# Opening of a conditioned hybrid layer: scale and shift made in two halves, conditioning blocks reordered, first projection weights split early

## What is computed (the reference, cut)

```python
mod = silu(c) @ w_ada + b_ada              # 9 conditioning rows (8 sample, 1 prompt), w_ada 1024 x 6144
sh1, sc1, g1, sh2, sc2, g2 = split(mod, 6)
h = rmsnorm(x, norm_mix_g) * (1 + sc1) + sh1
proj = h @ w_in                            # q, f, i, g, conv B, conv C, conv v, two merge gates
```

## Time and profile before

| what | value |
|---|---|
| median of three runs | 2126.03 us (2125.35 to 2129.06) |
| the profiled execution's own time | 2128.7 us |
| its span | 2127.1 us |
| mean granted clock of PE, share of full speed | 0.957 |
| PE busy over the span | 1928.6 us (91%) |
| DVE, ACT, POOL busy | 1044.8, 872.1, 414.0 us (49%, 41%, 19%) |

### The profile page before, as it was taken

The page is one execution under the profiler, slowest core; times in us unless marked ns, Lnnn a source line. Parts: engine busy times, 40 slices in busy tenths (PEclk is TensorE's granted clock), DMA queues, the critical chain, the costliest instruction groups (busy, mean ns, idle before and its releaser), DMA issues. The chain is left out here.

```text
span 2127.1 us, 33716 instructions
## 1 busy us (share of the span) xinstructions
PE 1928.6 (91%) x10176; PEld 1507.9 (71%) x10177; DVE 1044.8 (49%) x1519; ACT 872.1 (41%) x1181; POOL 414.0 (19%) x337
## 2 busy tenths in 40 slices
PE   3799999899899999989789999999899999999960
PEld 3799999899888666755446777666566777777740
DVE  3212411155337334545336666565566666666646
ACT  4210111234203222211246666666566666666642
POOL 0100000111111000001112333333233333223320
PEclk9899999999899999999899999999999999999985
DMA  6211221011263666325069999999999999979946
GB/s 240 71 50 40 82 96 30 30 60 43 68 209 117 216 219 212 138 86 195 19 257 380 306 292 294 356 318 379 374 327 345 286 286 286 275 233 310 279 91 259
DMA packets 154836, 433.67 MB, mean 204 GB/s; under 512 B 11551, under 2 KB 76307, under 8 KB 130210
## 3 DMA queue, kind: packets, MB, share of 16 engines
q1 hardware_dynamic: 120338, 307.40, 38.6%
q0 software_dynamic: 31776, 116.05, 21.1%
q10 hardware_dynamic: 2672, 9.57, 1.2%
HBM read 351.27 MB, written 81.72 MB: 204 GB/s over the span
## 5 line engine op out<-in xcount | busy, mean ns | idle before, releaser
L2038 DVE TENSOR_TENSOR wexp_lo<-wexp,wexp_hi 128x2048 fp32r<-128x2048 f32 x190 | 426.9, 2289 | 49.3 <-ACT wexp_hi L1990 44.4
L1990 ACT ACTIVATE wexp_hi<-wexp 128x2048 fp32r x190 | 353.2, 1907 | 54.4 <-issue 52.9
L1971 PE MATMUL bank<-wexp_down,hTe 128*128 x736 | 331.0, 592 | 1.8 <-ACT ob L2016 1.8
L1946 PE MATMUL bank<-wexp_hi,x_hi 128*128 128x512 f32 x744 | 300.0, 403 | 3.8 <-DVE wexp_lo L2038 3.8
L1946 PE MATMUL bank<-wexp_hi,x_lo 128*128 128x512 f32 x744 | 291.5, 392 | 0.0
L1946 PE MATMUL bank<-wexp_lo,x_hi 128*128 128x512 f32 x744 | 290.0, 390 | 0.0
L1920 POOL DMA_INDIRECT acc_d<-ob,ixs x92 | 153.0, 1663 | 599.8 <-DMA acc_d<-ob,ixs 290.9
L1971 PEld LDWEIGHTS bank<-wexp_down,hTe 128*128 128x128 f32 x736 | 138.8, 189 | 142.4 <-issue 135.5
L494 PE MATMUL bank<-hT_hi,w_hi 128*128 128x344 f32 x576 | 187.7, 326 | 3.3 <-DVE w_lo L578 3.3
L494 PE MATMUL bank<-hT_hi,w_lo 128*128 128x344 f32 x576 | 185.7, 322 | 0.0
L494 PE MATMUL bank<-hT_lo,w_hi 128*128 128x344 f32 x576 | 185.1, 321 | 0.0
(11 more groups left out here) (338 smaller groups left out, 2917.3 us busy)
## 6 DMA issues: line engine op xcount, KB each, us to landing
wexp<-in_w_exp_gate SPq DMA_DIRECT2D x64, 1024.0 KB
wexp<-in_w_exp_up SPq DMA_DIRECT2D x64, 1024.0 KB
wexp_down<-in_w_exp_down SPq DMA_DIRECT2D x64, 1024.0 KB
wada<-in_w_ada SPq DMA_DIRECT2D x12, 2048.0 KB, 10.9
w_raw<-in_w_in SPq DMA_DIRECT2D x44, 512.0 KB, 3.9
gates_d<-gst POOLq DMA_DIRECT2D x48, 172.0 KB, 2.1
gate<-gates_d SPq DMA_DIRECT2D x16, 516.0 KB, 5.5
xn<-in_x_prompt ACTq DMA_DIRECT2D x8, 512.0 KB
```

Source lines behind the costliest of these rows:

```text
L1946: last = pe.matmul(banks[0][:].rearrange("p (g n) -> p g n", g=2), stat[:, b, k, :], mov[:, b, :, k * FF:(k + 1) * FF], start=(k == 0 and ...
L1971: last = pe.matmul(banks[4 + half][:], hT[:, f, :], wdn[:, bass.ds(slot, 1), f, half * 512:half * 512 + 512].rearrange("p a n -> p (a n)") ...
L1990: act.activation(w_hi[:, b, g, :], wexp[:, bass.ds(e & (RING - 1), 1), g, :].rearrange("p a n -> p (a n)"), ACT.Copy).then_inc(whi_ok, 1)
L2038: dve.tensor_tensor(w_lo[:, b, g, :], wexp[:, bass.ds(e & (RING - 1), 1), g, :].rearrange("p a n -> p (a n)"), w_hi[:, b, g, :], ALU.subtr ...
```

## The change

It has five parts.
1. x squared tile by tile: each tile of x has its own semaphore, and ACT squares it as soon as it has landed.
2. Blocks of w_ada are loaded and used in the order 0, 2, 1, 3. The parameter rows are turned after the first of them, into another bank.
3. Scale and shift are made in two halves of four feature tiles. PE's order is: block 0, parameter rows, block 2, turn their mod tiles, feature tiles 0 and 1, block 1, feature tiles 2 and 3, block 3, turn its and block 1's mod tiles, the sample tokens, feature tiles 4 to 7. DVE and ACT take up the second half's scale and shift between feature tiles 3 and 4, and the sample tokens before the last two feature tiles.
4. The first 128 columns of w_in are loaded behind the last block of w_ada on SP's queue, rounded by POOL, and the subtraction is POOL's too. For that w_raw and the first two slots of w_hi and w_lo are allocated in the opening.
5. In `project_in` the first pass stands outside the loop, and the conv state is turned and copied after it, not before. The loop has one pass fewer.

The core of the diff:

```diff
+COLUMNS = (4, 5, 6, 3, 0, 1, 2)
...
+            BLOCKS = (0, 2, 1, 3)
...
-                    for n in range(2):
+                    for n in BLOCKS[0:2]:
                         sp.dma_start(wada[:, n], ada_v[:, :, n * 512:(n + 1) * 512]).then_inc(ada_in[n], 16)
...
-                    for n in range(2, FIRST):
+                    for n in BLOCKS[2:]:
                         sp.dma_start(wada[:, n], ada_v[:, :, n * 512:(n + 1) * 512]).then_inc(ada_in[n], 16)
+                    sp.dma_start(w_raw[:], w_in[:, :, COLUMNS[0] * W:COLUMNS[0] * W + P]).then_inc(w0_in, 16)
...
+                    pool.wait_ge(w0_in, 16)
+                    pool.tensor_copy(w_hi[0][:, 0], w_raw[:]).then_inc(w0_hi, 1)
+                    pool.wait_ge(w0_hi, 1)
+                    pool.tensor_tensor(w_lo[0][:, 0], w_raw[:], w_hi[0][:, 0], ALU.subtract).then_inc(w0_lo, 1)
...
-                    act.wait_ge(x_in, 16 * TILES)
                     for t in range(TILES):
+                        act.wait_ge(x_in[t], 16)
...
-                        if k + 1 < KD:
+                        if k + 1 < KD and k + 1 != KD // 2:
                             first_half(k + 1)
...
+                        if k + 1 == KD // 2:
+                            act.wait_ge(modT_ok, 2)
+                            first_half(k + 1)
+                        if k == 6:
+                            act.wait_ge(smp_ok, 1)
+                            act.activation(hT_hi[:, :, T:], hsmp[:], ACT.Copy).then_inc(smp_hi_ok, 1)
...
+                    cond(0)
+                    pe.wait_ge(par_in, 16 * 5)
+                    pe.transpose(banks[7][:, 0:NPAR], par_rows[:], ident[0:NPAR, 0:NPAR]).then_inc(par_T, 1)
+                    cond(1)
+                    turn_mod(0)
+                    pe.wait_ge(xn_ok, TILES)
+                    turn(0)
+                    turn(1)
+                    cond(2)
+                    turn(2)
+                    turn(3)
+                    cond(3)
+                    turn_mod(1)
...
+                    for k in range(4, KD):
+                        turn(k)
...
+                    condition_rows(0)
+                    condition_rows(1)
+                    shift_and_scale(0)
...
                     second_half(0)
                     for k in range(KD):
-                        if k + 1 < KD:
+                        if k + 1 == KD // 2:
+                            rest(k)
+                            condition_rows(3)
+                            shift_and_scale(1)
                             second_half(k + 1)
...
+                        else:
+                            if k + 1 < KD:
+                                second_half(k + 1)
+                            rest(k)
+                        if k == 1:
+                            condition_rows(2)
+                        if k == 4:
+                            dve.wait_ge(smp_ps, 1)
+                            s.link(dve.tensor_tensor(hsmp[:], banks[6][:, 0:KD * NS].rearrange("p (k c) -> p k c", c=NS),
+                                                     modT[:, KD:, 0:NS], ALU.mult))
+                            dve.tensor_tensor(hsmp[:], hsmp[:], modT[:, 0:KD, 0:NS], ALU.add).then_inc(smp_ok, 1)
```

and in `project_in`:

```diff
-            load(0)
             for u in range(1, UNITS + 1):
...
+            pool.sem_inc(hi_ok, 1)
+            for c in range(1, CH):
+                pool.wait_ge(raw_in, 16 * c)
+                pool.tensor_copy(w_hi[c // 2][:, c % 2], raw[:]).then_inc(hi_ok, 1)
+            with pool.Fori(1, PASSES) as i:
...
+            tensor_pass(0, 0)
             pe.wait_ge(cs_in, 16)
...
-            with pe.Fori(0, 6) as i:
+            with pe.Fori(1, 6) as i:
                 tensor_pass(i, i * PER)
...
-            for c in range(CH):
+            dve.sem_inc(w_ready, 1)
+            for c in range(1, CH):
                 rest(0, c)
```

More of the change, by code:

```diff
@@ L154, in layer @@
         hT_lo = sb("hT_lo", [P, KD, TT], F32R, split, "right")
+        w_raw = sb("w_raw", [P, KD, P], F32, split, "right")
+        early = top.enter_context(ExitStack())
+        w_hi = [sb("w_hi0", [P, 2, KD, P], F32R, early, "right")]
+        w_lo = [sb("w_lo0", [P, 2, KD, P], F32R, early, "right")]
         ada_v = a["w_ada"].rearrange("l (k p) n -> p (l k) n", p=P)
@@ L178, in layer @@
             rstd = sb("rstd", [P, TILES], ctx=c1)
-            par_in, c_in, b_in, x_in = sem("par_in"), sem("c_in"), sem("b_in"), sem("x_in")
+            par_in, c_in, b_in = sem("par_in"), sem("c_in"), sem("b_in")
+            x_in = [sem(f"x_in{t}") for t in range(TILES)]
+            w0_in, w0_hi, w0_lo = sem("w0_in"), sem("w0_hi"), sem("w0_lo")
             ada_in = [sem(f"ada_in{i}") for i in range(FIRST)]
@@ L186, in layer @@
             dve1, pool1 = sem("dve1"), sem("pool1")
[L187 removed]
+            smp_ps, smp_ok, smp_hi_ok, hi_ok, lo_ok = (sem(n) for n in ("smp_ps", "smp_ok", "smp_hi_ok", "hi_ok", "lo_ok"))
+            BLOCKS = (0, 2, 1, 3)
             O_G, O_LB, O_HG, O_CW, O_CB = 0, KD, KD + 2 * CH, KD + 2 * CH + H, KD + 2 * CH + H + 3 * CH
@@ L265, in _, with turn @@
                     pe.wait_ge(cT_cp, 1)
-                    def cond(n):
+                    def cond(x):
+                        n = BLOCKS[x]
                         pe.wait_ge(ada_in[n], 16)
[L269 to L284, removed]
+                        if x >= 2:
+                            pe.wait_ge(mod_ok, x - 1)
+                        condition(pe, banks[x % 2], wada[:, n]).then_inc(mod_ps, 1)
+                    def turn(k):
                         for half in range(2):
@@ L297, in _ @@
                                             ident[0:NS, 0:NS])
-                    last.then_inc(xT_ps, 1)
+                    last.then_inc(smp_ps, 1)
+                    for k in range(4, KD):
+                        turn(k)
                 @block.vector
@@ L316, in _ @@
                     dve.wait_ge(b_in, 64)
[L317 to L330, removed]
@@ L338, in second_half, with rest @@
                                           modT[:, k, NS:NS + 1], ALU.mult, ALU.add).then_inc(h_dve_ok, 1)
+                    def rest(k):
+                        dve.wait_ge(hi_ok, k + 1)
+                        dve.tensor_tensor(hT_lo[:, k, 0:T], hraw[:, k % 3, :], hT_hi[:, k, 0:T], ALU.subtract).then_inc(lo_ok, 1)
                     second_half(0)
                     for k in range(KD):
-                        if k + 1 < KD:
+                        if k + 1 == KD // 2:
+                            rest(k)
+                            condition_rows(3)
+                            shift_and_scale(1)
                             second_half(k + 1)
[L344 to L348, removed]
-                    dve.tensor_tensor(hsmp[:], hsmp[:], modT[:, 0:KD, 0:NS], ALU.add).then_inc(smp_ok, 1)
+                        else:
[9 more added lines that the diff above has]
+                            dve.tensor_tensor(hsmp[:], hsmp[:], modT[:, 0:KD, 0:NS], ALU.add).then_inc(smp_ok, 1)
                     dve.wait_ge(smp_hi_ok, 1)
@@ L373, in layer @@
                     project_in(nc, tidy, a, c4, sb, sem, banks, par, ident, w_in, hT_hi, hT_lo, qT, fT, gT, bT, vv, u_end, w_raw,
-                               g_d, b_d, (O_LB, O_CW, O_CB))
+                               w_hi, w_lo, g_d, b_d, (O_LB, O_CW, O_CB))
+                early.close()
                 next_stage()
@@ L426, in layer, with project_in @@
         final(nc, a, o, sb, sem, eps, mod_d, x2_d, acc_d)
-def project_in(nc, tidy, a, ctx, sb, sem, banks, par, ident, w_in, hT_hi, hT_lo, qT, fT, gT, bT, vv, u_end, raw, g_d, b_d, offsets):
+def project_in(nc, tidy, a, ctx, sb, sem, banks, par, ident, w_in, hT_hi, hT_lo, qT, fT, gT, bT, vv, u_end, raw, w_hi, w_lo,
+               g_d, b_d, offsets):
     O_LB, O_CW, O_CB = offsets
     cvT = sb("cvT", [P, CH, TT], ctx=ctx)
-    w_hi = sb("w_hi", [P, CH, KD, P], F32R, ctx)
-    w_lo = sb("w_lo", [P, CH, KD, P], F32R, ctx)
+    w_hi = w_hi + [sb("w_hi1", [P, 2, KD, P], F32R, ctx)]
+    w_lo = w_lo + [sb("w_lo1", [P, 2, KD, P], F32R, ctx)]
     cstT = sb("cstT", [P, CH, NS * 2], ctx=ctx)
@@ L497, in used @@
             def used(c, n=1):
-                pe.matmul(banks[7][:, 0:2], w_hi[:, c, 0, 0:P], w_hi[:, c, 0, 0:2], start=True, stop=True).then_inc(w_used, n)
+                one = w_hi[c // 2][:, c % 2, 0]
+                pe.matmul(banks[7][:, 0:2], one[:, 0:P], one[:, 0:2], start=True, stop=True).then_inc(w_used, n)
             def tensor_pass(i, first):
@@ L540, in _ @@
             act.activation(lbt[:, 0:2, :], lbt[:, 0:2, :], ACT.Exp).then_inc(lb_ok, 1)
-            act.wait_ge(cT_ps, 1)
-            act.activation(cstT[:].rearrange("p c n -> p (c n)"), banks[6][:, 0:CH * 2 * NS], ACT.Copy).then_inc(cT_ok, 1)
             def take(dst, func, first):
@@ L552, in _ @@
             take(bT, ACT.Copy, 0)
+            act.wait_ge(cT_ps, 1)
```

(1 more changed line is left out.)

33 lines of the change are left out of this document (18 added, 15 removed).

## The result

The changed kernel takes 2114.94 us (median of 4 runs, 2109.96 to 2119.33) against 2125.69 us for the kernel before: ratio 0.9946, interval 0.9928 to 0.9964. Measured a second time, together with some of the experiments, it came to 0.9946 again (0.9932 to 0.9959). That is about 11 us less, where 12.8 were forecast; the median forecast was 2113.2, in a range of 2110 to 2117. The profiled execution is the longest of the four: 2119.33 us.

The account below looks back on a forecast made before the run. The opening's chain (x, squares, xn, bias, blocks 2 and 3, modT, eight tiles, weights) sets project_in's first matmul, which carries everything behind it. -13.3 + 0.5 = -12.8 takes 2128.7 to 2115.9, median 2113.2; range 2110 to 2117.

Parts of the forecast that it names:

- The squares and xn: Opening, ACT and DVE: squares start as tiles land, ending near 21.9 and not 29.2; xn ends at 30.1.
- The rival of tiles landing together: Opening: tiles of x land nearly together, squares and xn end as before, everything 6.7 us later: 2119.9; chance 0.12.
- Half 0: Opening, first four feature tiles: scale and shift at 32.3, first hT_lo at 34.8, the fourth ending at 42.3.
- The 1.1 us lost on block 1: Opening, PE: block 1 takes 2.5 us, so tile 2 is turned at 37.1 where DVE wanted it at 36.0.
- the 0.3 us charged to DVE for POOL's subtraction: Opening: slowdown of DVE while POOL subtracts the first weights, 0.3 us with bounds 0 and 2.
- POOL's own length: Opening: POOL's 128x1024 subtraction takes 2.7 to 13.4 us by elements; the low end and a little more was taken.
- The last rival: Opening: POOL and DVE hold each other up, six hT_lo each cost 4.8 us more: 28.8, giving 2142; chance 0.02.
- Half 1: Opening, last four feature tiles: modT at 43.7, first hT_lo at 47.0, the eighth ending at 53.7, opening ending at 53.9.
- The clock part of the prediction: Start of project_in: PE again starts slowly at 1.2 GHz, as before the change; priced at nothing.
- The weights: Change of stage: load, rounding and subtraction gone from in front of PE, 0.9 us left; moved conv state costs 0.5.
- The clock at the start: project_in's first matmuls on PE: same slow start, priced at nothing; bounds 2.8 us less or 1.5 more.
- The sum: First matmul of project_in 13.3 us earlier, at 55.1 against 68.39; with 0.5 lost, 12.8 less in all.

Follow-up runs that it names:

- the version without stalls: e5_flow with the subtraction of the first weights on POOL again: 2113.19 us, ratio 0.9938 to the kernel before.
- e5_flow: Changed kernel with first weights subtracted on DVE, second scale and shift before the third hT_lo, PE's turns reordered, parameter rows after the second block: 2113.34 us, 0.9932.

## Why the prediction was right, and where not

**The squares and xn**: 30.1 forecast, 30.4 measured. That tiles land one after another was open; the rows of ACT show squares starting on arrival at 13.28, 15.32, 17.37 and 19.97, the last three or four some 2 us apart. The rival of tiles landing together is out.

**Half 0**: parameters at 27.5 (27.50 measured), scale and shift at 32.3 (32.84), first hT_lo at 34.8 (35.72; DVE waited 0.76 for transposes that I had priced at the high clock), the fourth ending at 42.3. That one ended at 45.17: 0.9 carried over and 2.0 from POOL. The 1.1 us lost on block 1 came out as 1.04 by two errors that cancel: tiles 0 and 1 took 2.29 us and not 1.84, the block 1.96 and not 2.5.

**The term that failed most is the 0.3 us charged to DVE for POOL's subtraction.** It had the bounds 0 and 2, and 2.0 is what it cost. I had reasoned that POOL would run in DVE's gap near 44; it ran at 40.83, as soon as its data was there, beside the third hT_lo: the weights had landed at 39.27 and not at 42.5, because I had added the whole time of a load (4.5 us) to the moment at which the queues are empty. POOL's own length was near the low end, as taken (3.27 for 2.7 forecast; 2.36 alone). The last rival, in which the engines hold each other up, named the right mechanism and a price far too large: only what overlaps is lost, one hT_lo and not six. The rule quoted from the Trainium skill ("GPSIMD Engine Reference", section 8) agrees with the traces, and the estimate of 2.25 us from its section 3.1 is near the 2.35 to 2.38 measured; I took the rule in and then priced what it says at 0.3.

**Half 1**: after the fourth hT_lo, 1.35 to scale and shift was forecast and 1.31 measured (45.17 to 46.48). From there to DVE's part of tile 4, 1.1 was forecast, for the sample tokens that come first; it was 2.38, since the transposes ran at 1.2 GHz. The clock part of the prediction looked only at the start of project_in and not at the gap that the change opens on PE in the middle of the opening. The experiment with PE kept busy gave back some 1.65.

**The weights**: 0.9 from the opening's end to the first matmul forecast, 0.96 measured; the conv state 0.5 forecast, 0.4 measured. The second block was covered as said: no wait of PE behind the first matmul.

**The clock at the start**: priced at nothing. The low clock lasted 4.5 us after the first matmul instead of 6.2, which is 6 matmuls at 0.158 and not at 0.287: 0.8 gained by chance; in the experiments it lasted between 3.0 and 6.1.

**The sum**: the first matmul came 9.3 us earlier and not 13.3. The 4.0 us missed are 0.9 at the start of half 0, 1.7 from POOL (2.0 for 0.3) and 1.3 before tile 4, to within 0.1. With the 0.4 and the 0.8 the 9.3 make 9.7, and the two profiled spans differ by 9.4. The medians differ by 10.8 and 11.0. The rest, some 1 us, is within what the stages behind differ by from run to run; no run settles it. So the mechanism was right, but that the median missed by only 1.7 us where the first matmul missed by 4.0 is in part luck.

**The parts together**, first matmul against 68.39: squares alone -1.3, halves alone +3.7, both -3.6; weights alone -4.7, weights and halves -4.7, all three -9.3, each give or take 1 (the -4.7 of the weights alone holds the 1.5 by which that opening was late, so that the change of stage itself gave 6.2; halves alone and both, the two with late weights, hold loads that took 1.3 and 1.1 us longer than before). The halves pay only with the early squares, and the early squares pay little without the halves, since then xn waits for block 3. The prediction costed them as one chain, which was right, and did not say that of the squares and the halves each alone is worth little or less than nothing.

## What to carry to other kernels

A stage that waits for two late inputs gains little from making either early unless the other is early too: work out the chain for each part alone before splitting. A step that is moved "beside other work" to another engine runs when its data arrives, not when there is room; look up what its neighbour reads at that moment, and where possible put it behind a wait that puts it in the gap. And where an edit opens a pause on PE ahead of small transposes, price them at the low clock.

## What the runs showed of the hardware

- POOL's subtraction of two 128x1024 float32 tiles took 2.35 to 2.38 us where DVE was in no step on two SBUF tiles when it began and began none in its first 1.1 us, and 3.21 to 3.27 where an hT_lo had begun 0.1 to 0.4 us before it; that hT_lo took 3.23 to 3.38 instead of 1.22. Both together ran 40.68 to 44.10 in the changed kernel: 3.42 us, near the sum of the two alone (3.6). So both were held up there, the one that began first too. Where DVE's step began later (1.15 us after POOL's in the version without stalls, 2.0 after it with the squares late), POOL kept its time and DVE's step was longer by the overlap or a little less. DVE steps that read a bank kept their 0.80.
- POOL's rounding, with one tile read, was held up too: 1.04 us alone, and 1.47 where it began 0.58 us before the end of DVE's second hT_lo (1.21 with 0.32 us left, 1.53 with 0.64).
- 32 transposes of 128x128 float32 took 3.67 to 3.71 us at a granted clock of 1.00 (2.4 GHz) and 5.0 to 6.3 where PE had paused for 3.0 or 5.0 us before them and the clock rows read 0.50 (1.2 GHz) for part of them; with the subtraction on DVE the pause was 3.0 and the 32 took 5.99. With the halves alone the clock fell only after PE had begun again (1.00 until 53.0, the transposes from 52.66 on: 5.38).
- One block of 64 small matmuls took 1.95 to 1.98 us at its fastest and 3.64 at its slowest. At 37.88 in the run with the squares alone the slow pace (3.53) goes with a clock row of 0.50. In the first 34 us it is also found at a reading of 1.00: the second block took 3.64 with the parameter rows later, with PE kept busy and in e5_flow, and 1.96 in e5_flow's twin with the subtraction on POOL. No run explains this.
- After the stage's change, the load of 0.5 MB in 512-byte rows took 4.5 us before and with the squares alone, and 5.6 and 5.8 in the two kernels with halves and late weights. No run says why.
